# Row-block order 3, 1, 2, 0 with a lag of three steps in two causal attentions, and the forget gate's columns inside the first value chunk

## The chip, the cores and the metric

One core of a Trainium2 chip runs the whole program. The metric is the device time of one execution in microseconds, median of the runs. Engines: TensorE (PE) multiplies and transposes; VectorE (DVE) and ScalarE (ACT) compute elementwise and read the accumulators (PSUM banks); GpSimd (POOL) computes elementwise in SBUF; the SP queue issues the loads. All float32.

## The reference, cut to what matters

Two transformer blocks over 512 tokens of width 1024, batch 1. The change is in the first block:

```python
proj = h @ w_in            # q_a k_a v_a z_a q_b k_b v_b z_b (512 columns each), f_logit (8), g_logit (2048)
# per head (8 heads of 64), 128 query rows at a time, keys up to the block's end (causal)
z = q_a @ k_a.T / 8                                   # stick-breaking attention
log_1m = where(s < t, log_sigmoid(-z), 0)
after = cumsum(log_1m, reverse=True) - log_1m
y_a = where(s < t, exp(log_sigmoid(z) + after), 0) @ v_a
F = cumsum(log_sigmoid(f_logit + b_forget))           # over tokens, per head
y_b = softmax(q_b @ k_b.T / 8 + F[t] - F[s], s <= t) @ v_b    # forgetting attention
y_a, y_b = y_a * silu(z_a), y_b * silu(z_b)           # then output projections, gates, merge
```

Row block b (rows 128b to 128b+127) sees b+1 blocks of keys.

## The kernel before, in words

**Weights.** All weight matrices stream in chunks through three raw slots. For every product `mm3` (L448) does three matmuls, high x high, high x low and low x high; ScalarE makes the high part of a chunk (`split_weights`, L1086, the instruction is L1104), POOL the low part as a difference of two SBUF tiles (`low_weights`, L2294, the instruction is L2301, a quarter of a chunk each). SP loads a slot when it is used up (`chunk_in`, L2346; from chunk 12 on in a loop, L2389). All matmuls have the line L425, all transposes ("turns") L432.

**Before the attentions** TensorE makes q_a, k_a, v_a (in rows: `project_rows`, L504, with chunk 12 the first of two), z_a, q_b and k_b. ScalarE or VectorE move each tile out of its bank (`move`, L1137 and L1810). Then 24 matmuls of 8 x 512 (L604 to L609) make f_logit from w_f, whose parts were split early (L1163, L1786). ScalarE takes it through Abs, Exp and Ln (L1278 to L1285), VectorE through a maximum and a scan over the tokens (L1833, L1834).

**The attentions.** Four head pairs times four row blocks are 16 steps of each; the 32 run in one loop on every engine, step n having pair n // 4 and block n % 4, so lengths 1, 2, 3, 4. On TensorE (L671) step i does in this order:

- the scores of step i (`head_scores`, L621), into one of two pairs of banks, which must be free;
- the turns of the weights of step i - LAG, LAG = 2 (`head_turns`, L635), into the one pair of banks for turns;
- side work: half a tile of the projections v_b, z_b and g (`side`, L658): 18 matmuls of 256 columns or 9 of 512 in an even step, 30 or 15 in an odd one, all into the one bank 7;
- the values of step i - LAG (`head_values`, L644), which need the turned weights copied to SBUF.

ScalarE in the first attention (`stick_step`, L1299): in even steps the side tile's copy, then Abs, Exp, Ln of the scores of i (L1309 to L1311), then the Exp of step i - 1 (L1317) once VectorE is done with it; in steps 4k and 4k+1 half a weight split (L1325, L1327), and in the later even ones the silu of z_b. VectorE (`stick_step`, L1839): after the last block of a pair the gating product (L1845), then the copy of the turned weights of i - LAG (L1812), then the chain of step i: maximum and sum (L1856), two scans from the right, one a head (L1859), and the difference (L1861), which frees the score banks. In even steps from 10 on the silu product (L1817).

In the second attention VectorE does a reduce that also gives the row's extremum (L1891) and the scaling by the reciprocal sum (L1900, L1903), ScalarE the Exp (L1361) and the copy of the turned weights (L1141), beside the gates' work. Weights stand in `pairs`, four slots in the first attention and three in the second; the turned weights in two slots `ptb`. After the last values eight tiles of g follow (L694).

Of the kernel before, what the change touches and what calls it, by code (L numbers as in the profile page):

```python
# [7 lines left out]
F32 = mybir.dt.float32  # L8
# [21 lines left out]
LAG = 2  # L30
SLOTS_A, SLOTS_B = 4, 3
# [25 lines left out]
EARLY_CHUNKS = 12  # L57
# [7 lines left out]
for _n, _c in (("c", 8), ("b_ada", 24), ("norm_g", 8), ("b_gate", 16), ("final_g", 8), ("mix_g", 8),  # L65
# [3 lines left out]
               ("conv_b", 22), ("b_forget", 1), ("w_f", 64), ("lora", 256), ("g2", 256), ("pool_w", 256)):  # L69
# [3 lines left out]
NCOLS = PARAM_COLS["w_f"][0]  # L73
LATE_PARAM = PARAM_COLS["lora"][0]
# [61 lines left out]
def build(nc, x_in, mem_in, params_in, consts_in, ada_in, stream_in, down_in, out, x2_kept, kx_kept, vx_kept, nF_kept):  # L136
    with ExitStack() as ctx:
# [79 lines left out]
        w_raw, w_lo = sb_both("weights", RAW, CHUNK_F)  # L217
        w_hi = sb("weights_high", HI, CHUNK_F, kind=F32R)
# [3 lines left out]
        wf_hi = sb("w_f_high", 64, kind=F32R)  # L222
        wf_lo = sb("w_f_low", 64, kind=F32R)
# [75 lines left out]
        pairs, ptb = at(W1, SLOTS_A, 2, T), at(W1 + 4096, 2, 2, T)  # L299
# [78 lines left out]

        def raw_of(c):
            return h_slots[0][c] if c < 2 else w_raw[:, c % RAW, :]  # L380

        def lo_of(c):
            return h_slots[1][c] if c < 2 else w_lo[:, c % RAW, :]

        def hi_of(c):
            return h_slots[2][c % 2] if c in (0, 1, 4, 5) else w_hi[:, c % HI, :]
# [34 lines left out]
        def _(pe):  # L421
# [82 lines left out]
            def project_rows(key, first, last, lhs, blocks):  # L504

                for i in range(first, last):
                    c, b = divmod(i, blocks)
                    if b == 0:
                        chunk[0] = next_chunk(KD, 256)
# [85 lines left out]
            project_rows("va", 0, 2 * NB, hrow, NB)  # L595
# [39 lines left out]
            def head_turns(tag, n, slots, weights_done):  # L635

                pe.wait_ge(weights_done, n + 1)
                o = TR2.take(pe, ("T" + tag, n))
                for hh in range(2):
                    for s in range(n % NB + 1):  # L640
                        turn(o[hh][:, P * s:P * (s + 1)], pairs[:, n % slots, hh, P * s:P * (s + 1)],
                             TR2.filled if hh and s == n % NB else None)

            def head_values(tag, n, v):  # L644

                pair, b = divmod(n, NB)
                TR2.wait_out(pe, ("T" + tag, n))
                if b == 0:
                    PV.take(pe, ("y" + tag, pair))
                y = bank[6]  # L650
                for s in range(b + 1):
                    for hh in range(2):
# [3 lines left out]
                           PV.filled if b == NB - 1 and s == b and hh else None)  # L656
# [415 lines left out]
        def _(act):  # L1072
# [13 lines left out]
            def split_weights(part=0, parts=1):  # L1086
# [7 lines left out]
                n = (CHUNK_F if c < STREAM else DOWN_K * P) // parts  # L1094
# [68 lines left out]
            high(wf_hi, par("w_f", 0, 64), sem("wf_hi"))  # L1163
# [121 lines left out]
            nc.scalar.activation(fa, fa, ACT.Ln, bias=1.0).then_inc(sem("f_ln"), 1)  # L1285

# [12 lines left out]
            def stick_step(i):  # L1299
# [13 lines left out]
                if 0 <= n < N:  # L1313
                    end = P * (n % NB + 1)
                    M2.wait_out(act, ("a", n))
                    w = pairs[:, n % SLOTS_A, :, 0:end]
# [30 lines left out]
            def fox_step(i):  # L1347
# [4 lines left out]
                if 0 <= n < N:  # L1352
                    end = P * (n % NB + 1)
                    move(("Tb", n), ptb[:, n % 2, :, 0:end], lambda o: o[:, :, 0:end], TR2)
                if i < N:
                    end = P * (i % NB + 1)
                    M2.wait_out(act, ("b", i))
                    for hh in range(2):
                        c = 2 * (i % SLOTS_B) + hh
                        w = pairs[:, i % SLOTS_B, hh, 0:end]  # L1360
                        nc.scalar.activation(w, w, ACT.Exp, scale=-1.0, bias=small[:, 8 + c:9 + c],  # L1361
                                             accum_out=small[:, 14 + c:15 + c]).then_inc(sem("fox_exp"), 1)
# [340 lines left out]
        def _(dve):  # L1703
# [80 lines left out]
            dve.wait_ge(sem("wf_hi"), 1)  # L1784
            tt(gmix[:, :], par("final_g", 0, 8), par("mix_g", 0, 8), ALU.mult)
            tt(wf_lo, par("w_f", 0, 64), wf_hi.bitcast(F32), ALU.subtract).then_inc(sem("wf_split"), 1)  # L1786
# [41 lines left out]
            for m in range(4):  # L1828
                move(("kb", m), kb[:, m, :])

# [4 lines left out]
                .then_inc(sem("nF_ready"), 1)  # L1835


            N = PAIRS * NB
            def stick_step(i):  # L1839
# [7 lines left out]
                if 0 <= n < N:  # L1847
                    end = P * (n % NB + 1)
                    move(("Ta", n), ptb[:, n % 2, :, 0:end], lambda o: o[:, :, 0:end], TR2)
                if i < N:  # L1850
                    end = P * (i % NB + 1)
                    o = M2.full(dve, ("a", i))
                    w = pairs[:, i % SLOTS_A, :, 0:end]
# [660 lines left out]
```

## Time and profile before

| | us |
|---|---|
| median of 3 runs | 1319.56 (1319.38 to 1319.75) |
| the profiled execution | 1318.44 |
| its span | 1316.6 |
| TensorE busy | 1269.6 (96%) |
| VectorE busy | 638.0 (48%) |
| ScalarE busy | 543.6 (41%) |
| POOL busy | 538.7 (41%) |

The profile is one execution. "Busy" is the time with an instruction running; a row of the timeline gives start, length, engine, line, operation, the tiles by name, how many were merged (x), and in brackets the idle time before it with what ended it. A merged group runs in each step: its length is that of all of them. Matmuls are pipelined: the next one starts before the last one's end, so costs on TensorE are differences of starts. The first attention's scores start at 218.7 us, the second's at about 306, and the tiles of g after both at 390.0.

### The profile page before, as it was taken

What the parts mean: (1) busy time and instruction counts of PE and PEld (TensorE: products, weight loads), DVE (VectorE), ACT (ScalarE), POOL (GpSimd) and SP (SyncE); (2) the same over time, 40 slices, a digit from 0 to 9 for tenths busy, and PEclk for the clock granted to TensorE, in tenths of its full rate; (3) what the DMA queues carried; (4) which work ended last, traced back from release to release, by engine and by line L of the source; (5) the groups of instructions that cost most, each with busy time, mean ns of one, the idle gap of its engine ahead of it and who ended that gap; (6) DMA issues with size and microseconds to landing.
All of it is one profiled execution on the core that took longest, in us unless ns stands there. A gap on an engine that the chain in (4) does not pass through costs nothing.

```text
span 1316.6 us, 19858 instructions
## 1 busy us (share of the span) xinstructions
PE 1269.6 (96%) x8194; PEld 1007.3 (77%) x8194; DVE 638.0 (48%) x995; ACT 543.6 (41%) x834; POOL 538.7 (41%) x432
## 2 busy tenths in 40 slices
PE   6999999999999999999999899999999999999999
PEld 5778887766768888766787667778788888888887
DVE  4450002886440166696448647265565656562000
ACT  5541434676665233463544444353422323221111
POOL 6554443131333454364142126421455555544443
PEclk9999999999999999999999999999999999999999
DMA  9835221202112222421220023300222222222223
GB/s 391 331 138 194 97 96 65 81 33 81 64 65 91 87 88 91 186 87 64 80 91 5 3 82 120 150 33 32 96 96 97 96 96 96 96 76 88 88 88 108
DMA packets 20549, 133.26 MB, mean 101 GB/s; under 512 B 2280, under 2 KB 2408, under 8 KB 7408
## 3 DMA queue, kind: packets, MB, share of 16 engines
q1 hardware_dynamic: 18720, 119.50, 25.4%
q10 hardware_dynamic: 1744, 12.53, 2.5%
q8 instruction: 65, 1.06, 0.3%
q14 instruction: 20, 0.16, 0.0%
HBM read 125.71 MB, written 6.31 MB: 100 GB/s over the span
## 4 chain that ended last, share of the span: by engine, by line
PE 86%; DVE 8%; ACT 4%; issue 2%; DMA 0%; POOL 0%; SPq 0%; ACTq 0%; DVEq 0%
PE banks L425 84%; PE banks L432 2%; DVE arena L2005 1%; DVE arena L1859 1%; ACT arena L1141 1%; DVE arena L1969 1%; DVE arena L2004 0%; ACT arena L1310 0%; ACT arena L1309 0%; DMA arena<-in_mem 0%; DVE arena L1812 0%; DVE arena L1856 0%; ACT arena L1311 0%; DVE arena L2031 0%; DVE arena L2030 0%
## 5 line engine op out<-in xcount | busy, mean ns | idle before, releaser
L2301 POOL TENSOR_TENSOR weights_low<-weights,weights_high 128x512 fp32r<-128x512 f32 (+1 forms) x388 | 498.5, 1316 | 669.7 <-ACT weights_high L1104 669.7
L425 PE MATMUL banks<-h_high_low,weights_high 128*128 128x512 f32 x880 | 356.0, 405 | 2.4 <-POOL weights_low L2301 1.3
L425 PE MATMUL banks<-h_high_low,weights_low 128*128 128x512 f32 x880 | 347.6, 395 | 0.0
L425 PE MATMUL banks<-h_low,weights_high 128*128 128x512 f32 x880 | 347.5, 395 | 0.0
L1104 ACT ACTIVATE weights_high<-weights 128x2048 fp32r<-128x2048 f32 (+2 forms) x105 | 178.2, 1697 | 343.4 <-PE banks L425 331.0
L425 PEld LDWEIGHTS banks<-h_high_low,weights_high 128*128 128x128 f32 x880 | 165.2, 188 | 48.4 <-issue 7.1
L425 PEld LDWEIGHTS banks<-h_low,weights_high 128*128 128x128 f32 x880 | 165.2, 188 | 41.0 <-issue 2.9
L425 PEld LDWEIGHTS banks<-h_high_low,weights_low 128*128 128x128 f32 x880 | 164.9, 187 | 40.4
L425 PE MATMUL banks<-arena 64*64 64x64 f32 (+4 forms) x1288 | 104.8, 280 | 15.1 <-DVE arena L1812 6.4
L425 PEld LDWEIGHTS banks<-arena 64*64 64x64 f32 (+3 forms) x1288 | 73.8, 152 | 37.4 <-issue 17.9
L1939 DVE TENSOR_TENSOR xres<-banks,xres 128x512 f32<-128x512 f32 x24 | 16.6, 690 | 141.2 <-PE banks L425 141.2
L425 PE MATMUL banks<-gact_high,weights_high 128*128 128x512 f32 x176 | 69.6, 396 | 0.0
L425 PE MATMUL banks<-gact_low,weights_high 128*128 128x512 f32 x176 | 69.6, 396 | 0.0
L425 PE MATMUL banks<-gact_high,weights_low 128*128 128x512 f32 x176 | 69.6, 395 | 0.0
L1141 ACT ACTIVATE arena<-banks 128x256 f32<-128x256 f32 (+4 forms) x82 | 41.6, 519 | 66.6 <-PE banks L432 33.6
L1812 DVE COPY arena<-banks 128x256 f32<-128x256 f32 (+3 forms) x40 | 25.4, 635 | 78.1 <-PE banks L425 74.3
L425 PE MATMUL banks<-weights_high,h_high_low 128*128 128x256 f32 x192 | 55.1, 287 | 0.3 <-ACT arena L1141 0.3
L425 PE MATMUL banks<-weights_low,h_high_low 128*128 128x256 f32 x192 | 53.9, 281 | 0.0
L425 PE MATMUL banks<-weights_high,h_low 128*128 128x256 f32 x192 | 53.9, 281 | 0.0
L2273 DVE TENSOR_TENSOR arena<-banks,sums 128x512 f32<-128x512 f32 x22 | 15.2, 692 | 77.3 <-PE banks L425 72.2
L1124 ACT ACTIVATE sums<-xres 128x512 f32<-128x512 f32 x32 | 20.2, 632 | 70.4 <-DVE xres L1939 39.4
L432 PE MATMUL banks<-consts,arena 128*128 128x128 f32 x245 | 38.0, 281 | 2.8 <-DVE arena L2231 2.7
(347 smaller groups left out, 2045.6 us busy)
## 6 DMA issues: line engine op xcount, KB each, us to landing
weights<-in_stream SPq DMA_DIRECT2D x83, 1024.0 KB, 4.9
weights<-in_down SPq DMA_DIRECT2D x16, 704.0 KB, 4.0
arena<-in_ada SPq DMA_DIRECT2D x8, 1024.0 KB, 12.3
arena<-in_ada SPq DMA_DIRECT2D x8, 512.0 KB, 7.3
h<-in_stream SPq DMA_DIRECT2D x2, 1024.0 KB, 9.1
xres<-in_x SPq DMA_DIRECT2D x1, 2048.0 KB, 28.5
x_kept<-xres ACTq DMA_DIRECT2D x1, 2048.0 KB, 6.3
xres<-x_kept ACTq DMA_DIRECT2D x1, 2048.0 KB, 7.8
```

Source lines behind the costliest of these rows:

```text
L425: ins = nc.tensor.matmul(o, lhsT, rhs, start=start, stop=stop, skip_group_check=skip)
L432: ins = nc.tensor.transpose(o, i, ident[0:rows, 0:rows])
L1104: nc.scalar.activation(hi_of(c)[:, cols], raw_of(c)[:, cols], ACT.Copy)\
L1124: nc.scalar.activation(SQ[n][i % 2][:, 0:width], src[:, k, 0:width], ACT.Square)\
L1141: nc.scalar.activation(dst, s_, ACT.Copy).then_inc(ring_.out(key), 1)
L1812: nc.vector.tensor_copy(dst, o if src is None else src(o)).then_inc(ring_.out(key), 1)
L1859: ins = nc.vector.tensor_tensor_scan(v, ones(end), v, 0.0, ALU.mult, ALU.add)
L1939: ins = tt(xres[:, m, :], o, xres[:, m, :], ALU.add)
L1969: tt(dst, o, zscale, ALU.mult).then_inc(M.out(key), 1)
L2005: stt(zm[:, m, :], zdiff, par("mu", m), z[:, 1:T + 1], ALU.mult, ALU.add).then_inc(sem("zm"), 1)
L2273: tt(a[:, 2:T + 2], o, rms[:, :], ALU.mult).then_inc(M.out(("up", m, 0)), 1)
L2301: nc.gpsimd.tensor_tensor(lo_of(c)[:, cols], raw_of(c)[:, cols], hi_of(c)[:, cols].bitcast(F32), ALU.subtract).then_inc(sem("weights_split ...
```

## The change

- `ROW_ORDER = (3, 1, 2, 0)`: in both attentions the blocks of a pair go in this order, so lengths 4, 2, 3, 1, on every engine; the first block of a pair in the new order does the pair's waits, the last one signals its end.
- LAG = 3; four slots of weights in both attentions (the fourth is in `sums`).
- The eight columns of w_f lie behind the first 256 columns of v_a: chunk 12 has 264 columns per row tile. Its 96 matmuls make 264 columns; ScalarE copies the last eight of each of the four row tiles to `f_cols` and waits for that copy before the main one. After q_b TensorE turns the four [128 x 8] tiles into f_logit's [8 x 512] (before k_b). The 24 matmuls and the split of w_f are gone.
- ScalarE's forget chain comes before two weight splits, VectorE's before the four moves of k_b.
- SP issues chunks 12 to 14 by hand, before the late parameters; slot 0 of the weights is 2112 columns wide and the others 2048.

```diff
-LAG = 2
-SLOTS_A, SLOTS_B = 4, 3
+LAG = 3
+SLOTS_A, SLOTS_B = 4, 4
+ROW_ORDER = (3, 1, 2, 0)
...
-EARLY_CHUNKS = 12
+EARLY_CHUNKS = 15
+WITH_F, F_WIDE = 12, 256 + HEADS
...
-        pairs, ptb = at(W1, SLOTS_A, 2, T), at(W1 + 4096, 2, 2, T)
+        pairs = [at(W1 + 1024 * i, 2, T) for i in range(3)] + [sums[:, 0:2, :]]
+        ptb = at(W1 + 4096, 2, 2, T)
...
-            def project_rows(key, first, last, lhs, blocks):
+            def project_rows(key, first, last, lhs, blocks, wide=256):
...
+                    n = wide if c == 0 else 256
...
-                        mm3(o[:, 0:256], lhs(k, b), [p_[:, k, :] for p_ in w], k == 0, k == KD - 1,
+                        mm3(o[:, 0:n], lhs(k, b), [p_[:, k, :] for p_ in w], k == 0, k == KD - 1,
...
             project("qb", 4, KD, h, T)
+            o = M.take(pe, "f")
+            pe.wait_ge(sem("f_cols"), NB)
+            for b in range(NB):
+                turn(o[0:HEADS, P * b:P * (b + 1)], f_cols[:, b, :], M.filled if b == NB - 1 else None)
             project("kb", 4, KD, h, T)
-            o = M.take(pe, "f")
-            pe.wait_ge(sem("wf_split"), 1)
-            wf = [v.rearrange("p (k n) -> p k n", k=KD) for v in (wf_hi, wf_lo)]
-            for k in range(KD):
-                mm3(o[0:HEADS, :], [v[:, k, :] for v in wf], h(k), k == 0, k == KD - 1,
-                    M.filled if k == KD - 1 else None)
...
-                pair, b = divmod(i, NB)
-                if b == 0:
+                pair, b = i // NB, ROW_ORDER[i % NB]
+                if i % NB == 0:
...
                 for i in range(first, last):
                     c, b = divmod(i, NB)
+                    if c == 0:
+                        o = M.full(act, (key, c, b))
+                        nc.scalar.activation(f_cols[:, b, :], o[:, 256:F_WIDE], ACT.Copy).then_inc(sem("f_cols"), 1)
+                        act.wait_ge(sem("f_cols"), b + 1)
...
-            for _ in range(2):
-                split_weights()
-
             o = M.full(act, "f")
             fx, fa = z_gate[0:HEADS, 0, :], z_gate[0:HEADS, 1, :]
+            act.wait_ge(sem("silu"), 4)
...
             nc.scalar.activation(fa, fa, ACT.Ln, bias=1.0).then_inc(sem("f_ln"), 1)
+            for _ in range(2):
+                split_weights()
...
-                    end = P * (i % NB + 1)
-                    e = pairs[:, i % SLOTS_A, :, 0:end]
+                    end = P * (ROW_ORDER[i % NB] + 1)
+                    e = pairs[i % SLOTS_A][:, :, 0:end]
...
-            for m in range(4):
-                move(("kb", m), kb[:, m, :])
-
             fx, fa = z_gate[0:HEADS, 0, :], z_gate[0:HEADS, 1, :]
             dve.wait_ge(sem("f_ln"), 1)
             link(stt(fx, fx, 0.0, fa, ALU.max, ALU.add))
             nc.vector.tensor_tensor_scan(nF[0:HEADS, :], ones(T, HEADS), fx, 0.0, ALU.mult, ALU.add)\
                 .then_inc(sem("nF_ready"), 1)
+            for m in range(4):
+                move(("kb", m), kb[:, m, :])
...
-            for c in range(8, EARLY_CHUNKS):
+            for c in range(8, WITH_F):
                 chunk_in(c)
             for k in range(ADA_RING, KD):
                 gate_in(k)
+            for c in range(WITH_F, EARLY_CHUNKS):
+                chunk_in(c)
             sp.dma_start(params[:, LATE_PARAM:], params_in[:, LATE_PARAM:]).then_inc(sem("late_loaded"), 16)
```

## Rows read from the trace of the kernel before

**Rows 1.** The page: the chain of work that ended last, shares of the span by engine.

```profile
PE 86%; DVE 8%; ACT 4%; issue 2%; DMA 0%; POOL 0%; SPq 0%; ACTq 0%; DVEq 0%
```

**Rows 2.** Who TensorE waited for: total, times, longest (whole span; then 365.5 to 389).

```profile
PE banks L425 <- DVE arena L1812: 6.4, 4, 2.0
...
PE banks L425 <- ACT arena L1141: 2.0, 2, 1.1
```

**Rows 3.** TensorE by 2 us windows: length, busy (count), granted clock, DMA share, GB/s.

```profile
282.00:284.00 2.00, 0.23 (x4) 1.00 0.21 86
...
304.00:306.00 2.00, 0.10 (x2) 1.00 0.25 102
306.00:308.00 2.00, 2.00 (x18) 0.67 0.00 0
308.00:310.00 2.00, 2.00 (x11) 0.50 0.03 8
```

**Rows 4.** Timeline of TensorE: four turns; first and last of 24 forget matmuls.

```profile
166.76 0.60 PE L432 MATMUL banks<-consts,arena 128*128 128x128 f32 x4
167.12 0.48 PE L425 MATMUL banks<-h_high_low,weights_high 128*128 128x512 f32 x1
...
212.00 0.39 PE L425 MATMUL banks<-h_high_low,w_f_high 128*8 128x512 f32 x1
...
217.32 0.40 PE L425 MATMUL banks<-h_high_low,w_f_low 128*8 128x512 f32 x1
```

**Rows 5.** Timeline of TensorE in the second period of the first attention.

```profile
241.82 1.04 PE L432 MATMUL banks<-consts,arena 128*128 128x128 f32 x8
...
242.62 0.36 PE L425 MATMUL banks<-weights_high,h_high_low 128*128 128x256 f32 x1
...
246.35 1.94 PE L425 MATMUL banks<-arena 128*64 128x128 f32 x20
...
248.35 0.39 PE L432 MATMUL banks<-consts,arena 128*128 128x128 f32 x2
248.49 0.36 PE L425 MATMUL banks<-weights_high,h_high_low 128*128 128x256 f32 x1
...
250.79 1.50 PE L425 MATMUL banks<-arena 128*64 128x128 f32 x8
...
252.34 0.61 PE L432 MATMUL banks<-consts,arena 128*128 128x128 f32 x4
```

**Rows 6.** Timeline: ScalarE starts a 3-block step; VectorE's copy behind its chain.

```profile
227.16 0.81 ACT L1309 ACTIVATE arena<-banks 128x768 f32<-128x768 f32 x1 [0.47 <-PE banks L425]
...
233.54 0.68 DVE L1812 COPY arena<-banks 128x512 f32<-128x512 f32 x1
```

**Rows 7.** The chain of waits, 252 to 262 us, a 4-block step: start, length, what.

```profile
252.54 1.03 ACT arena L1309
...
254.69 1.07 ACT arena L1311
...
257.11 2.35 DVE arena L1859 x2
...
260.63 0.96 DVE arena L1812
...
261.63 0.43 PE banks L425 x3
```

**Rows 8.** Timelines of ScalarE, VectorE and POOL where VectorE and POOL meet.

```profile
243.31 0.64 ACT L1311 ACTIVATE arena<-arena 128x512 f32<-128x512 f32 x1
...
244.78 2.34 DVE L1859 TENSOR_TENSOR_SCAN arena<-consts,arena 128x256 f32<-128x256 f32 x2
...
245.28 2.90 POOL L2301 TENSOR_TENSOR weights_low<-weights,weights_high 128x512 fp32r<-128x512 f32 x2 [1.30 <-ACT weights_high L1104]
...
312.50 2.61 DVE L1903 TENSOR_SCALAR arena<-arena,small 128x128 f32<-128x128 f32 x2
...
312.51 2.51 POOL L2301 TENSOR_TENSOR weights_low<-weights,weights_high 128x512 fp32r<-128x512 f32 x2 [2.91 <-ACT weights_high L1104]
```

More of the change, by code:

```diff
@@ L72 @@
 NPARAM = _at
-NCOLS = PARAM_COLS["w_f"][0]
-LATE_PARAM = PARAM_COLS["lora"][0]
+NCOLS = LATE_PARAM = PARAM_COLS["lora"][0]
 CONST_COLS = {}
@@ L638, in head_turns @@
                 o = TR2.take(pe, ("T" + tag, n))
+                b = ROW_ORDER[n % NB]
                 for hh in range(2):
-                    for s in range(n % NB + 1):
-                        turn(o[hh][:, P * s:P * (s + 1)], pairs[:, n % slots, hh, P * s:P * (s + 1)],
-                             TR2.filled if hh and s == n % NB else None)
+                    for s in range(b + 1):
+                        turn(o[hh][:, P * s:P * (s + 1)], pairs[n % slots][:, hh, P * s:P * (s + 1)],
+                             TR2.filled if hh and s == b else None)
             def head_values(tag, n, v):
-                pair, b = divmod(n, NB)
+                pair, b = n // NB, ROW_ORDER[n % NB]
                 TR2.wait_out(pe, ("T" + tag, n))
-                if b == 0:
+                if n % NB == 0:
                     PV.take(pe, ("y" + tag, pair))
@@ L655, in head_values @@
                            ptb[:, n % 2, hh, P * s:P * (s + 1)], s == 0, s == b,
-                           PV.filled if b == NB - 1 and s == b and hh else None)
+                           PV.filled if n % NB == NB - 1 and s == b and hh else None)
             def side(i):
@@ L1093, in split_weights @@
                     return
-                n = (CHUNK_F if c < STREAM else DOWN_K * P) // parts
+                n = width_of(c) // parts
                 cols = slice(n * part, n * (part + 1))
@@ L1313, in stick_step @@
                 if 0 <= n < N:
-                    end = P * (n % NB + 1)
+                    end = P * (ROW_ORDER[n % NB] + 1)
                     M2.wait_out(act, ("a", n))
-                    w = pairs[:, n % SLOTS_A, :, 0:end]
+                    w = pairs[n % SLOTS_A][:, :, 0:end]
                     nc.scalar.activation(w, w, ACT.Exp).then_inc(sem("stick_w"), 1)
@@ L1359, in fox_step @@
                         c = 2 * (i % SLOTS_B) + hh
-                        w = pairs[:, i % SLOTS_B, hh, 0:end]
+                        w = pairs[i % SLOTS_B][:, hh, 0:end]
                         nc.scalar.activation(w, w, ACT.Exp, scale=-1.0, bias=small[:, 8 + c:9 + c],
-                                             accum_out=small[:, 14 + c:15 + c]).then_inc(sem("fox_exp"), 1)
+                                             accum_out=small[:, 16 + c:17 + c]).then_inc(sem("fox_exp"), 1)
                 if i in (5, 9):
@@ L1847, in stick_step @@
                 if 0 <= n < N:
[L1848 removed]
+                    end = P * (ROW_ORDER[n % NB] + 1)
                     move(("Ta", n), ptb[:, n % 2, :, 0:end], lambda o: o[:, :, 0:end], TR2)
                 if i < N:
[L1851 removed]
+                    end = P * (ROW_ORDER[i % NB] + 1)
                     o = M2.full(dve, ("a", i))
[L1853 removed]
+                    w = pairs[i % SLOTS_A][:, :, 0:end]
                     dve.wait_ge(sem("stick_ln"), i + 1)
@@ L1879, in fox_step @@
                 if i < N:
-                    pair, b = divmod(i, NB)
-                    end = P * (b + 1)
-                    if b == 0:
+                    pair = i // NB
+                    end = P * (ROW_ORDER[i % NB] + 1)
+                    if i % NB == 0:
                         dve.wait_ge(sem(f"nF{pair % 2}_loaded"), 16 * (pair // 2 + 1))
@@ L1890, in fox_step @@
                         c = 8 + 2 * (i % SLOTS_B) + hh
-                        ins = nc.vector.tensor_tensor_reduce(pairs[:, i % SLOTS_B, hh, 0:end], o[:, hh, 0:end],
+                        ins = nc.vector.tensor_tensor_reduce(pairs[i % SLOTS_B][:, hh, 0:end], o[:, hh, 0:end],
                                                              nF_bc[pair % 2][:, hh, 0:end], -1.0, 3.0e38, ALU.add, ALU.min,
@@ L1896, in fox_step @@
                 if 0 <= n < N:
-                    end = P * (n % NB + 1)
+                    end = P * (ROW_ORDER[n % NB] + 1)
                     c = 2 * (n % SLOTS_B)
                     dve.wait_ge(sem("fox_exp"), 2 * n + 2)
-                    link(nc.vector.reciprocal(small[:, 48 + c:50 + c], small[:, 14 + c:16 + c]))
+                    link(nc.vector.reciprocal(small[:, 48 + c:50 + c], small[:, 16 + c:18 + c]))
                     for hh in range(2):
-                        w = pairs[:, n % SLOTS_B, hh, 0:end]
+                        w = pairs[n % SLOTS_B][:, hh, 0:end]
                         ins = ts(w, w, small[:, 48 + c + hh:49 + c + hh], None, ALU.mult)
```

51 lines of the change are left out of this document (27 added, 24 removed).

## The prediction

> **What bounds the kernel now.** I read the page's chain of waits first, then who waited for whom on TensorE (PE), then the timelines of the three engines in both attentions. TensorE is 86% of the chain that ended last [rows 1]: time is gained only where TensorE gets less to do or waits less. In the region that the change touches it waits for VectorE's copies L1812 four times, 6.4 us in all, twice 2.0 and so twice about 1.2, all in the first (stick-breaking) attention; and twice for ScalarE's copies at the end of the second, 2.0 us in all [rows 2]. Inside the second attention there is no such wait. So 8.4 us of waiting can be won there at most, plus what the clock cost: behind one of the two 2.0 us waits the granted clock was 0.67 for 2 us and 0.50 (the 1.2 GHz level) for 2 more, which loses 0.66 + 1.0 = 1.7 us; behind the other, just as long, it stayed at 1.00 [rows 3].
>
> **Part 1, the forget gate.** Removed: 24 matmuls of 512 columns, started 212.00 to 217.32, 23 steps of 0.231, so 5.55 us of TensorE [rows 4]. Added: the 96 matmuls of the first value chunk go from 256 to 264 columns. Twelve 256-column matmuls are the difference between the long and the short side part, 3.73 and 2.30 us (from the starts 242.62, 246.35, 248.49, 250.79), so 0.119 each [rows 5]; 512 columns take 0.231, so a column costs 0.44 ns and the eight more cost 96 x 3.5 ns = 0.34 us. Four turns of [128 x 8]: four full turns took 166.76 to 167.12, 0.36 us, and 0.1 more for the refilled pipe [rows 4]. Bounds of this part: 4.5 (if turns and wide matmuls cost twice as much) and 5.1. I take 5.55 - 0.34 - 0.46 = **-4.8 us**.
>
> What rides along is covered. ScalarE's four small copies with a wait each stand beside row tiles of 24 x 0.119 = 2.8 us of TensorE, of which ScalarE's one copy fills a small part; the split of chunk 12 is 3% longer. If the cover were gone the four would cost under 0.81 us each, what ScalarE takes for 768 columns of a bank [rows 6]. ScalarE's forget chain now runs while TensorE works on the first key tile (24 x 0.231 = 5.6 us), and the two weight splits queued behind it are not wanted before the side work. VectorE's max and scan go ahead of the four key copies; the last of these, which releases the bank that the first scores take, is not late. The SP queue issues chunks 12 to 14 by hand in the old order; the late parameters come behind them and are first read hundreds of microseconds later. The removed high/low split of w_f was off the chain: nothing gained.
>
> **Part 2, order and lag.** Numbers of a step n mean: position 4k holds 4 blocks, 4k+1 two, 4k+2 three, 4k+3 one. TensorE's work is the same; what counts is where VectorE's copy of the turned weights (L1812, three steps late) stands: in program order behind the whole chain of the step before. A 4-block chain runs from Abs at 252.54 over the scans at 257.11 to the copy at 260.63, and TensorE goes on at 261.63: 9.09 us, here with a 3-block copy [rows 7]. In the new order the 3-block copy of 4k+2 stands behind the chain of 4k+4 likewise. TensorE meanwhile does: turns of 2, side 2.30, values 2 with scores 2, turns of 3, side 3.73. Turns go from 0.14 (1 block) to 0.80 (4), so 0.36 and 0.58; values and scores together 2.00 for 7 blocks and 1.55 for 5, so 1.33 for 4 [rows 5]. Sum 8.30: a wait of **0.8** each period, three times, 2.4. The 4-block copy of 4k stands behind the 3-block chain of 4k+2: 227.16 to 233.54 is 6.38 [rows 6], with the gating product (0.6, an estimate: two thirds of the 0.96 of a 768-column copy [rows 7]) and the copy itself (1.2, estimate from the same) 8.2 to 8.3; TensorE does 0.14 + 2.30 + 0.88 + 0.80 + 3.73 = 7.85: **0.4**, three times, 1.3 with the first pair's smaller one. The silu products of the last periods delay VectorE as they do now, by 0.8 (from 1.2 to 2.0 [rows 2]), at three of these places: 2.4. Sum 6.1 against 6.4 now: the order moves the waits, it doesn't remove them.
>
> At the start the first chain is now a long one. Scores of step 2 need the bank that step 0's chain releases, 8.2 us after its scores; TensorE has 2.30 + 0.73 + 3.73 = 6.8 to do: 1.5 us. Then step 2's side work wants the side bank, whose ScalarE copy is queued behind the exponential of the long block: 0.6. Start: **+2.1**. At the end three steps of turns and values stand without side work, not two, with a ScalarE copy before each and gate work between: bounds 2.0 (as now) and 3.3 (three of the longest, 1.1 [rows 2]); I take 2.9, **+0.9**. Attention without anything else: 6.1 + 2.1 + 2.9 - 8.4 = **+2.7**, bounds +1.7 and +4.
>
> **The collision.** ScalarE splits a half chunk right after the Ln and a short Exp of each step 4k and 4k+1, and POOL then runs two subtractions. Now 4k is the shortest step; in the new order it is the 4-block one, on the chain that TensorE waits for. In the trace scan pairs that meet POOL are slow: two 256-column scans took 2.34 while POOL's pair took 2.90 from 245.28 [rows 8], where two 512-column scans took 2.35 undisturbed, so about 1.2 was expected [rows 7]. The loss of 1.1 costs nothing today (VectorE waits for ScalarE afterwards). Where POOL asked within 0.01 us of VectorE (312.51, 312.50), two tiny products took 2.61 [rows 8]. Timing of the meeting: with the same short Exp between, POOL starts 245.28 - 243.95 = 1.33 us after Ln's end [rows 8]; the long block's scans start 257.11 - 255.76 = 1.35 after it [rows 7]. They meet head on, in three periods (k = 1 to 3). Price per meeting 1.1 (scan first, one subtraction in between) to 2.3 (both scans held). I take 1.5, nearer the low end since the starts are a tie: **+4.5**, bounds 3.4 and 6.9.
>
> The Trainium skill, SBUF — State Buffer, section Who interferes with whom, says that VectorE with two SBUF inputs and GpSimd share one pair of ports by an exclusive lock, and the loser is blocked for the whole instruction. The rows above agree; it speaks against this change, and by it the scans (constant ones and a tile) are always hit, the copies from PSUM never. Without the rule and its rows the sum would stand at -2.1 before the clock.
>
> **Clock.** The waits at 4k+2 become 2.3, 2.3 and about 3. A 2.0 us wait lowered the clock once in two [rows 3]. Between 0 and three or four losses of 1.7; I take two, 3.4, against 1.7 now: **+1.7**. The Trainium skill, TensorE: Matmul & The Clock Gate, section What's actually happening, calls the observation free-running, which would make the count a matter of phase; the two equal waits agree.
>
> **Sum.** -4.8 + 2.7 + 4.5 + 1.7 = +4.1 us. The profiled execution took 1318.44 (span 1316.6), 1.1 below the median of the runs, 1319.56; I lay the difference on both: 1322.5 for a profiled one, **1323.7** for the median.
>
> **The rivals.** (1) *No collision on the chain*, faster: VectorE and POOL slip past each other (ScalarE's Exp ahead of the split is held, or the scans come first and POOL's pair fits behind). Then -4.8 + 2.7 and the clock between 0 and -1.7: -2.9, **1316.7**. For it: the tie is 0.02 us wide. Against: POOL's pair lasts 2.5 us and the scans 2.35, so they overlap unless one is 2 us off. It decides when the extra per period is under about 0.3. (2) *The third step of slack covers every copy*, as the lag suggests: -4.8 - 6.4 - 1.7 + 0.9 = -12, **1307.6**. Against it: a later use doesn't help a copy whose place in VectorE's queue moved just as far; it would need chains 2 us shorter than those of [rows 6, 7]. (3) *The small collision*: 1.1 a meeting and one drop of the clock: -4.8 + 2.7 + 3.4 + 0 = +1.3, **1320.9**, no difference.
>
> **How the numbers follow.** A measurement of this kernel tells 0.2%, 2.6 us, from no change. Collision with its price near or over my value: 0.50, slower. Rival 3: 0.25, same. Rival 1: 0.18, of which 0.13 faster and 0.05 same. Rival 2: 0.07, faster. So faster 0.20, same 0.30, slower 0.50. Range: the collision's upper bound with two drops is 1319.56 - 4.8 + 2.7 + 6.9 + 1.7 = 1326.1, with one more drop 1327.8; below it reaches rival 1: 1316.5 to 1327.5. Of the cases with a collision alone it would be 1320.5 to 1327.5. Outside stay rival 2, the clock-free half of rival 1 and a tail above, under 0.2.
>
> **What would show it.** Right: the forget matmuls gone and the first scores 4.8 us earlier; waits for L1812 at the values of 4k+2 of 2 us and more from the second pair on, 0.8 in the first; L1859 pairs of 512 columns at 3.4 to 4.6 us beside L2301 three times, 2.35 the first time; a bank wait of 1.5 us before the third scores; three waits at the end; granted clock 0.5 behind some of them. Wrong: 512-column scans all at 1.2, or L1812 waits under 3 us in all.

## The result, and the profile after

The changed kernel took 1328.76 us (median of six runs, 1325.78 to 1331.14), the kernel before in the same comparison 1319.95 (1319.38 to 1322.32). The ratio is 1.006, 95% interval 1.0048 to 1.0072: about 8 us slower, where +4.1 was forecast. No run lies near the median: three took 1325.78 to 1326.96 us and three 1330.57 to 1331.14. The profiled execution took 1326.96 with a span of 1325.4, 8.8 us above the span before. Three landmarks split these 8.8 us (us from the start of the span):

| | first scores | first g tile behind both attentions | end | start moved | attentions | rest |
|---|---|---|---|---|---|---|
| before | 218.72 | 389.99 | 1316.6 | | 171.3 | 926.6 |
| after | 214.27 | 394.71 | 1325.4 | -4.45 | 180.4 (+9.2) | 930.7 (+4.1) |

The chain of work that ended last is still TensorE's, with a point more of VectorE, against [rows 1]:

```profile
PE 84%; DVE 9%; ACT 4%; issue 2%; DMA 0%; POOL 0%; SPq 0%; ACTq 0%; DVEq 0%
```

Who TensorE waited for between 205 and 312 us of the changed kernel, and then between 385 and 402 (total, times, longest), against 6.4 and 2.0 in [rows 2]:

```profile
PE banks L433 <- DVE arena L1822: 12.8, 7, 3.7
PE banks L433 <- DVE arena L1871: 1.6, 1, 1.6
PE banks L433 <- ACT arena L1149: 0.4, 1, 0.4
```

```profile
PE banks L433 <- ACT arena L1149: 2.5, 3, 1.4
```

L1822 is the copy that was L1812. Of its 12.8 us, 1.0 stands before the first scores, where the kernel before waited 1.0 for ScalarE. So 16.4 us of waiting stand in the attentions, in 11 waits, where 8.4 stood in 6. The three largest are the ones behind the long chains. Timeline of VectorE in the changed kernel, around the second long block and then the two later ones:

```profile
220.22 2.37 DVE L1869 TENSOR_TENSOR_SCAN arena<-consts,arena 128x512 f32<-128x512 f32 x2
...
238.67 1.22 DVE L1866 SCALAR_TENSOR_TENSOR arena<-banks,arena 128x1024 f32<-128x1024 f32 x1 [2.17 <-ACT arena L1323]
239.93 4.51 DVE L1869 TENSOR_TENSOR_SCAN arena<-consts,arena 128x512 f32<-128x512 f32 x2
244.47 1.23 DVE L1871 TENSOR_TENSOR arena<-banks,arena 128x1024 f32<-128x1024 f32 x1
245.61 0.95 DVE L1822 COPY arena<-banks 128x768 f32<-128x768 f32 x1
...
263.81 4.51 DVE L1869 TENSOR_TENSOR_SCAN arena<-consts,arena 128x512 f32<-128x512 f32 x2
...
288.30 4.52 DVE L1869 TENSOR_TENSOR_SCAN arena<-consts,arena 128x512 f32<-128x512 f32 x2
```

And the same moment on ScalarE, POOL and TensorE:

```profile
237.51 1.06 ACT L1323 ACTIVATE arena<-arena 128x1024 f32<-128x1024 f32 x1
...
238.47 0.40 ACT L1329 ACTIVATE sums<-sums 128x256 f32<-128x256 f32 x1
238.78 1.04 ACT L1112 ACTIVATE weights_high<-weights 128x1024 fp32r<-128x1024 f32 x1
...
239.90 3.45 POOL L2311 TENSOR_TENSOR weights_low<-weights,weights_high 128x512 fp32r<-128x512 f32 x2 [19.51 <-ACT weights_high L1112]
...
246.61 1.72 PE L433 MATMUL banks<-arena 128*64 128x128 f32 x16 [3.00 <-DVE arena L1822]
...
270.50 1.72 PE L433 MATMUL banks<-arena 128*64 128x128 f32 x16 [3.13 <-DVE arena L1822]
...
295.60 2.38 PE L433 MATMUL banks<-arena 128*64 128x128 f32 x16 [3.75 <-DVE arena L1822]
```

Read it from the right: TensorE has stood 3.00 us when the copy of 245.61 is through; that copy is queued behind the whole chain, and in the chain two scans take 4.51 us that took 2.37 the first time, where POOL's last subtraction ended 0.2 us after their start. POOL starts its two subtractions at 239.90, 0.03 us ahead of the scans. The same happens in each of the three later periods: 2.15 us each, 6.5 in all.

The start and the end show the smaller terms, TensorE's timeline again:

```profile
223.90 0.92 PE L433 MATMUL banks<-arena 64*128 64x384 f32 x4 [1.58 <-DVE arena L1871]
...
225.47 0.39 PE L433 MATMUL banks<-weights_high,h_high_low 128*128 128x256 f32 x1 [0.44 <-ACT arena L1149]
...
389.80 0.66 PE L433 MATMUL banks<-arena 128*64 128x128 f32 x8 [0.69 <-ACT arena L1149]
...
392.63 0.88 PE L433 MATMUL banks<-arena 128*64 128x128 f32 x12 [1.36 <-ACT arena L1149]
...
394.34 0.44 PE L433 MATMUL banks<-arena 128*64 128x128 f32 x4 [0.47 <-ACT arena L1149]
```

The clock, in 2 us windows (length; busy time and count of TensorE's matmuls, its weight loads, VectorE, ScalarE and POOL; granted clock, DMA share, GB/s), fell once behind the longest wait, and once where it had not before, in the second block of the program, far behind the change:

```profile
294.00:296.00 2.00, 0.40 (x8) 0.40 (x10) 2.00 (x4) 1.89 (x2) 0.00 (x0) 1.00 0.02 4
296.00:298.00 2.00, 2.00 (x16) 0.76 (x13) 1.97 (x3) 0.60 (x2) 1.81 (x2) 0.63 0.03 8
298.00:300.00 2.00, 2.00 (x8) 1.71 (x9) 1.49 (x3) 1.62 (x2) 1.55 (x1) 0.52 0.00 0
...
716.00:718.00 2.00, 2.00 (x62) 1.88 (x66) 0.99 (x2) 1.89 (x5) 0.00 (x0) 0.59 0.00 0
718.00:720.00 2.00, 2.00 (x64) 1.66 (x60) 1.52 (x6) 0.00 (x0) 0.00 (x0) 0.56 0.03 8
```

The two windows of each lose 0.74 + 0.96 = 1.7 us and 0.82 + 0.88 = 1.7 us.

### The profile page after: what moved, and what is told of

Its sections match the earlier page's. It is cut to its first block, busy times and chain, and to the rows that moved or that the text cites. A ratio compares the mean times of both kernels' runs of the same rounds, so it can differ in the third digit from the quotient of the medians.

```text
span 1325.4 us, 19815 instructions
## 1 busy us (share of the span) xinstructions
PE 1270.3 (96%) x8174; PEld 1010.1 (76%) x8174; DVE 640.1 (48%) x994; ACT 543.4 (41%) x837; POOL 542.9 (41%) x432
## 4 chain that ended last, share of the span: by engine, by line
PE 84%; DVE 9%; ACT 4%; issue 2%; DMA 0%; POOL 0%; SPq 0%; ACTq 0%; DVEq 0%
PE banks L433 83%; DVE arena L1869 2%; PE banks L440 1%; DVE arena L2015 1%; ACT arena L1149 1%; DVE arena L1822 1%; DVE arena L1866 1%; ACT arena L1322 1%; ACT arena L1323 1%; DVE arena L1979 1%; ACT arena L1321 0%; DVE arena L2014 0%; DMA arena<-in_mem 0%; DVE arena L2041 0%; DVE arena L2040 0%
## 5 line engine op out<-in xcount | busy, mean ns | idle before, releaser
L2311 POOL TENSOR_TENSOR weights_low<-weights,weights_high 128x512 fp32r<-128x512 f32 (+2 forms) x388 | 502.8, 1329 | 672.2 <-ACT weights_high L1112 672.2
L1112 ACT ACTIVATE weights_high<-weights 128x2048 fp32r<-128x2048 f32 (+3 forms) x105 | 178.3, 1698 | 341.5 <-PE banks L433 341.5
L433 PE MATMUL banks<-arena 64*64 64x64 f32 (+6 forms) x1288 | 104.7, 280 | 21.6 <-DVE arena L1822 12.8
L1149 ACT ACTIVATE arena<-banks 128x512 f32<-128x512 f32 (+5 forms) x82 | 41.5, 518 | 52.9 <-PE banks L440 29.4
L433 PE MATMUL banks<-weights_high,h_high_low 128*128 128x256 f32 (+1 forms) x192 | 55.3, 288 | 0.7 <-ACT arena L1149 0.7
L433 PE MATMUL banks<-weights_low,h_high_low 128*128 128x256 f32 (+1 forms) x192 | 54.2, 282 | 0.0
L433 PE MATMUL banks<-weights_high,h_low 128*128 128x256 f32 (+1 forms) x192 | 54.2, 282 | 0.0
L1822 DVE COPY arena<-banks 128x256 f32<-128x256 f32 (+3 forms) x40 | 25.3, 633 | 55.7 <-PE banks L433 46.8
L433 PEld LDWEIGHTS banks<-gact_low,weights_high 128*128 128x128 f32 x176 | 33.0, 188 | 8.6
## 6 DMA issues: line engine op xcount, KB each, us to landing
arena<-in_ada SPq DMA_DIRECT2D x8, 1024.0 KB, 11.9
```

Source lines behind the costliest of these rows:

```text
L433: ins = nc.tensor.matmul(o, lhsT, rhs, start=start, stop=stop, skip_group_check=skip)
L1112: nc.scalar.activation(hi_of(c)[:, cols], raw_of(c)[:, cols], ACT.Copy)\
L1149: nc.scalar.activation(dst, s_, ACT.Copy).then_inc(ring_.out(key), 1)
L1822: nc.vector.tensor_copy(dst, o if src is None else src(o)).then_inc(ring_.out(key), 1)
L2311: nc.gpsimd.tensor_tensor(lo_of(c)[:, cols], raw_of(c)[:, cols], hi_of(c)[:, cols].bitcast(F32), ALU.subtract).then_inc(sem("weights_split ...
```

## The experiments

The theory, **collision**: POOL's two subtractions and the scans of the long block meet head on in three periods, which costs 2.15 us each plus what the longer waits take from the clock; the row order does nothing else of weight (too strong, as experiments 1 and 3 show), and the third step of lag gives nothing, since the copy moved just as far in VectorE's queue (**queue**). The rivals: the meeting is incidental, and the order or ScalarE's split on the long chain is to blame; or the lag is what costs or helps. Unless another base is named, an edit is made to the changed kernel. Ratios are to the kernel before.

**1. The splits moved.** Only the first half chunk's split leaves the step of the long block for the end of the step before it, in both attentions:

```diff
-                if i % 4 == 0 and 4 <= i <= N:
+                if i % 4 == 3 and i < N:
                     split_weights(0, 2)
```

> The changed kernel with one thing moved on ScalarE: the first half of each weight split in the attentions goes from step 4k to the end of step 4k-1, so that POOL's two subtractions are over before the scans of the 4-block step; the second half stays in 4k+1. Theory 'collision': the three scan pairs of 4.51 us are 2.35 again, the copies L1822 are waited for 0.8 to 1.5 us instead of 3.0, 3.1 and 3.7, the clock's drop near 296 us goes with them: about 7 to 10 us under the changed kernel, 0.996 to 1.000 of the kernel before. Rival 'order and lag alone' (the long chain and its queued copy make the waits, POOL has no part): waits of 3 us stay, ratio 1.005 to 1.007.

Measured: 1320.76 us, ratio 1.0001 (0.9991 to 1.001). VectorE's timeline, and then who TensorE waited for (205 to 402 us):

```profile
239.20 2.34 DVE L1869 TENSOR_TENSOR_SCAN arena<-consts,arena 128x512 f32<-128x512 f32 x2
```

```profile
PE banks L433 <- DVE arena L1822: 7.1, 7, 1.6
PE banks L433 <- ACT arena L1149: 3.0, 4, 1.2
PE banks L433 <- DVE arena L1871: 1.6, 1, 1.6
```

All four long pairs are back at 2.3 to 2.4, and 5.7 of the 12.8 us of waiting for the copy are gone. Moving POOL's work off the long scans is worth 0.6%, about 8 us, as much as the changed kernel had lost. The waits give 5.6 of these 8 (17.4 and 11.7 us between 205 and 402), and the profile has no loss of the clock before 1315 us, where the changed kernel's had two.

**2. The same move in the kernel before.** If moving the split is good in itself, it is good here too; if it is the meeting that counts, the move should now do harm, since the long block stands at 4k+3.

> The same move in the kernel before (order 0, 1, 2, 3, lag 2). There step 4k+3 is the 4-block one, so the move puts POOL's pair onto its scans. Theory 'collision': four scan pairs of 512 columns at 3.5 to 4.6 us, L1812 waited for 2 us and more in the first periods too, 4 to 8 us slower, ratio 1.003 to 1.006. Rival 'order and lag alone': nothing changes, ratio 0.999 to 1.001.

Measured: 1328.85 us, ratio 1.0054 (1.0041 to 1.0067). VectorE's scans and POOL's pair:

```profile
235.20 3.39 DVE L1859 TENSOR_TENSOR_SCAN arena<-consts,arena 128x512 f32<-128x512 f32 x2
...
235.84 3.82 POOL L2301 TENSOR_TENSOR weights_low<-weights,weights_high 128x512 fp32r<-128x512 f32 x2 [17.06 <-ACT weights_high L1104]
```

The edit that mends the changed kernel spoils the old one: in all four periods the long pair takes 3.4 us. Here the first scan is already running when POOL asks, and one subtraction gets in between, +1.05; in the changed kernel POOL is first, and two get in, +2.15. The meeting is not all of this loss, though. The waits for the copies L1812 grew by 2.5 us (6.4 to 8.9), those for ScalarE in the attentions by 3.0 (2.0 to 5.0; its split moved in the second attention too), and the clock was lost three times instead of once. What the meeting alone costs here was not separated.

**3. The forget gate alone**, and **4. the order, lag and slots alone.** The first is the changed kernel with the old values of the constants; the second is the kernel before with the new ones.

```diff
-LAG = 3
-SLOTS_A, SLOTS_B = 4, 4
-ROW_ORDER = (3, 1, 2, 0)
+LAG = 2
+SLOTS_A, SLOTS_B = 4, 3
+ROW_ORDER = (0, 1, 2, 3)
```

> Only the forget gate's part (columns inside the first value chunk, chains moved forward), with order 0, 1, 2, 3, lag 2 and 4 and 3 slots. Both theories: 4.8 us less TensorE work and the attentions as before: ratio 0.9958 to 0.9970, 1314 to 1316 us. If part of it comes back (later clock drops, or the key tiles' moves late) 0.997 to 0.999.

> Only the order 3, 1, 2, 0 with lag 3 and four slots, the forget gate as before. Theory 'collision': 9 us longer attentions by the three waits, the start and the end, and the clock: ratio 1.008 to 1.012. If the two parts work on each other (rival: the earlier start shifts ScalarE's split onto the scans) it would be less, 1.002 to 1.006, and the scan pairs would be 2.35 to 3.5.

Measured: the forget gate 1318.66 us, 0.9971 (0.996 to 0.9982), a gain of 3.8 us (2.7 by the medians, 1318.66 against 1321.38); order, lag and slots 1332.9 us, 1.0078 (1.0065 to 1.0091), a loss of 10.3. The product of the two ratios is 1.0049, the lower end of what both together gave: the parts don't act on each other in a way that shows. In the second the long scans stand at 4.51, 4.51 and 4.53 us, and TensorE waits 11.9 us for the copy. Experiment 1, measured beside experiment 3, says what order and lag cost without the meeting: 1.0001 against 0.9971, and the intervals don't touch. That is 2 to 4 us, and the profiles have 11.7 and 9.2 us of waiting (205 to 402 us).

**5. The lag alone, 6. the order without the lag.** Experiment 5 takes ROW_ORDER back to (0, 1, 2, 3) and leaves lag 3 and the four slots; experiment 6 leaves the new order and sets LAG = 2.

> The changed kernel with the old order 0, 1, 2, 3 and the lag of three kept: against the run with the forget part alone it adds only the lag. Theory 'queue' (the copy of the turned weights stands in VectorE's order behind the chain of the step before, so a later use moves its place too): one wait of about 1.5 us a pair at the 2-block values instead of the 3-block ones, scans of 4 blocks 2.35 us, the sum of VectorE waits 5 to 7 us as with lag two: ratio 0.996 to 0.998. Rival 'slack': the copy has a step more and the waits vanish, 0.991 to 0.993.

> The changed kernel with lag two: the order alone beside the forget part. Theory 'collision': the 4-block scans meet POOL three times (4.5 us), now one wait of 2.5 to 3.3 us a pair from the second on, at the 1-block values behind that chain; some 4 us over the forget part alone: ratio 1.000 to 1.004. Rival 'the lag does the harm': as the forget part alone, 0.996 to 0.998.

Measured: 5 took 1317.01 us, 0.998 (0.9967 to 0.9992), no better than the 0.9971 of experiment 3, which has lag 2 and three slots of weights in the second attention and is otherwise the same. A row of the waits (205 to 402 us) and one of TensorE's timeline say why: TensorE waits in every period again, and as long for the copy as with lag 2 (7.2 us in five waits in experiment 3):

```profile
PE banks L433 <- DVE arena L1822: 7.3, 6, 1.6
```

```profile
234.87 1.29 PE L433 MATMUL banks<-arena 128*64 128x128 f32 x12 [1.44 <-DVE arena L1822]
```

Experiment 6 took 1326.09 us, 1.0039 (1.0023 to 1.0055), with the three long pairs at 4.5 us: most of the loss belongs to the order, not to the lag. Against the change with lag 3 (1.006) the intervals overlap, so a cost of the third step is not shown by the times. The profiles have 12.9 us of waiting with lag 2 and 17.4 with lag 3 (205 to 402 us), so the third step adds waits beside the collision rather than covering them.

**7. Values alone a step later.** What would make a step of slack real? The copy must stand ahead of the next chain and its use a step behind it. So turns and copies stay two steps behind, and values alone go to three; the splits are moved as in experiment 1.

```diff
-LAG = 3
+LAG, VLAG = 2, 3
...
-            for i in range(2 * N + LAG):
+            for i in range(2 * N + VLAG):
...
-                elif n >= N:
+                elif N <= n < 2 * N:
                     head_turns("b", n - N, SLOTS_B, sem("fox_w"))
...
+                n = i - VLAG
                 if 0 <= n < N:
                     head_values("a", n, va)
```

(VectorE's two output gates and its loop take VLAG where they had LAG.)

> A version meant to beat both: order 3, 1, 2, 0, the turns two steps behind and only the values three, so that the copy between them has a step of its own, and the first half of the splits moved as in e1. Theory 'queue' plus 'collision': scans of 4 blocks 2.35 us, VectorE waits in the first attention under 2.5 us in all beside the 1.5 us at the start: ratio 0.991 to 0.994, 1309 to 1312 us. Rival: VectorE itself is full in the first attention (18 to 19 us of work in a pair of 20), so the waits only move: 0.996 to 0.998.

Measured: 1312.45 us, ratio 0.9935 (0.992 to 0.995), the fastest of all, 0.65% ahead of the kernel before. Who TensorE waited for, 205 to 402 us; L1823 is the copy:

```profile
PE banks L433 <- DVE arena L1872: 1.6, 1, 1.6
PE banks L433 <- DVE arena L1856: 1.1, 2, 0.8
PE banks L433 <- DVE arena L1823: 1.0, 1, 1.0
PE banks L440 <- issue: 0.7, 1, 0.7
PE banks L433 <- ACT arena L1150: 0.2, 1, 0.2
```

The one wait left for the copy is the 1.0 before the first scores. The attentions take 166.5 us (214.35 to 380.86), 4.8 less than before.

**8. The same with the old order, 9. POOL alone held back, 10. experiment 7 with the splits where they were.** Experiment 8 keeps the order (0, 1, 2, 3) and the splits. Experiment 9 asks which of the two partners of the meeting matters, ScalarE's split or POOL's subtractions: ScalarE does what it does in the changed kernel, and only POOL waits until the long chain has released its bank:

```diff
+                    if c in (22, 23, 24):
+                        M2.wait_out(pool, ("a", 4 * (c - 21)))
                     for i in range(PIECES):
```

> Order 0, 1, 2, 3 with turns two steps behind and values three, splits where they were, forget part kept. Theory 'queue': the waits of 1.1 to 2.0 us fall to under 0.5 each, the scans of 4 blocks stay clear of POOL; start without the bank wait; one longer wait where the second attention begins: ratio 0.992 to 0.995. Rival as in e7: 0.996 to 0.998.

> The changed kernel with POOL alone held: its subtractions of the chunks 22, 23 and 24 wait until VectorE has freed the scores of the 4-block steps 4, 8 and 12; ScalarE's and all other orders stay. Theory 'collision' (POOL's subtraction on the scans is the cost, not ScalarE's half split in that step): scan pairs 2.35 us, waits for L1822 0.8 to 1.6 us, ratio 0.999 to 1.001 like e1. Rival 'ScalarE's split is in the way': waits of 3 us stay, 1.005 to 1.007.

> As e7 (order 3, 1, 2, 0, turns two steps behind, values three) but with the half splits where the changed kernel has them. Theory 'collision': the 4-block scans take 4.5 us three times again, and since the chain also holds the score banks the slack for the copies doesn't help: TensorE waits about 1.8 us for the banks (L1872) three times and 0.7 for the side bank; 6 to 9 us over e7, ratio 0.998 to 1.001. Rival 'slack hides it': as e7, 0.993 to 0.995.

Measured: 8 took 1313.85 us, 0.9945 (0.993 to 0.996). So nearly all that experiment 7 gains comes with the old order as well; between the two the intervals overlap. Experiment 9 took 1319.39 us, 0.9995 (0.9983 to 1.0006), VectorE and POOL at the place where they met:

```profile
240.03 2.34 DVE L1869 TENSOR_TENSOR_SCAN arena<-consts,arena 128x512 f32<-128x512 f32 x2
...
243.71 5.77 POOL L2313 TENSOR_TENSOR weights_low<-weights,weights_high 128x512 fp32r<-128x512 f32 x4 [23.21 <-DVE arena L1871]
```

ScalarE's split still stands in the long chain's step, the scans take 2.34, and the loss is gone: it is POOL's subtractions beside the scans, not ScalarE's time. The meeting itself has only moved. The held subtractions now fall on the 256-column scans of the next step:

```profile
245.13 3.27 DVE L1869 TENSOR_TENSOR_SCAN arena<-consts,arena 128x256 f32<-128x256 f32 x2
```

These took 1.27 us at this place in the changed kernel, so 2.0 us are lost here, nearly as much as before. But this chain is short, and the waits for the copy fall from 12.8 us to 7.3 all the same. Experiment 10 took 1319.97 us, 0.9997 (0.9988 to 1.0006). The meeting costs the good version as much as it cost the change. VectorE and POOL:

```profile
240.43 4.51 DVE L1870 TENSOR_TENSOR_SCAN arena<-consts,arena 128x512 f32<-128x512 f32 x2
...
240.40 3.46 POOL L2312 TENSOR_TENSOR weights_low<-weights,weights_high 128x512 fp32r<-128x512 f32 x2 [19.38 <-ACT weights_high L1113]
```

And who TensorE waited for:

```profile
PE banks L433 <- DVE arena L1872: 6.5, 4, 1.7
```

The copy is in time now, so the chain's 2.15 us come out elsewhere: the scores wait for the bank that L1872 releases, four times instead of once.

**11, 12. Both kernels profiled again**, unedited, on one chip, for the 4.1 us of the rest that no term of mine had.

> The kernel before, profiled a second time on another chip; nothing is edited. Asked: the program behind both attentions was about 4 us longer in the one profile of the changed kernel (930.7 us from the first tile behind the attentions to the end, 926.6 before), which no part of the change explains. Theory 'kernel': the extra belongs to the changed program (its later part meets TensorE's unexplained waits, 3.6 us between 680 and 720 us against 1.4, and a second drop of the clock at 716 us), so this profile repeats 926.6 within 0.5 and 1.4. Rival 'execution': these waits and the clock vary from one execution to the next, and this profile shows 928 us or more and 2.5 us or more of such waits.

> The changed kernel, profiled a second time on the same chip as the kernel before; nothing is edited. Theory 'kernel': 930 to 931 us behind the attentions again, with the clock below 0.65 near 716 us. Rival 'execution': another sum; the clock falls elsewhere or once more. Either way the three pairs of 512-column scans take 4.5 us each, since instructions and their order are the same, and the wait for the copy behind them is 3.0 us or more each time.

Measured, one execution each: 1320.66 us (span 1318.8) and 1332.16 (span 1330.6). The attentions of the kernel before took 171.3 us again (219.19 to 390.48) and its rest 928.3, with 2.5 us of waits at 680 to 720 us that the profile doesn't explain, where the first profile had 1.4. The changed kernel's attentions took 185.2 us this time (215.22 to 400.40), its rest 930.2. Its long scans and the waits behind them repeat to the hundredth:

```profile
242.33 4.51 DVE L1869 TENSOR_TENSOR_SCAN arena<-consts,arena 128x512 f32<-128x512 f32 x2
...
249.01 2.04 PE L433 MATMUL banks<-arena 128*64 128x128 f32 x16 [3.00 <-DVE arena L1822]
```

The clock does not. Windows (columns as in the result) behind the first and the last of the five places where it fell between 226 and 404 us, one behind each of the five longest waits:

```profile
226.00:228.00 2.00, 1.57 (x7) 1.57 (x8) 1.40 (x3) 1.94 (x4) 0.00 (x0) 0.60 0.02 4
228.00:230.00 2.00, 2.00 (x12) 2.00 (x11) 1.03 (x2) 1.35 (x2) 0.00 (x0) 0.55 0.00 0
...
398.00:400.00 2.00, 1.53 (x12) 0.80 (x10) 0.00 (x0) 0.69 (x3) 2.00 (x2) 0.50 0.00 0
400.00:402.00 2.00, 2.00 (x8) 1.38 (x7) 1.48 (x3) 1.87 (x4) 1.43 (x2) 0.50 0.04 8
402.00:404.00 2.00, 2.00 (x7) 1.56 (x6) 2.00 (x4) 0.00 (x0) 0.00 (x0) 0.53 0.00 0
```

Its mean clock is 0.991, a loss of 0.009 x 1330.6 = 12 us, about seven times 1.7 (the last of the five places counts twice, and one more lies at 700.8 us), where the first profile lost 1.7 twice. The span grew by 5.2 only, about 1 us for each loss more. Waits that are 0.9 us shorter (16.5 against 17.4 us between 205 and 402) explain a part of that; the rest is open.

As for the rest of the program, part of its growth is a loss of the clock: in the second pair 1.7 us near 700 us and 1.7 more because the low stretch at 397 to 404 us reaches over the landmark at 400.40. But part belongs to the changed program. The same 1002 matmuls of the second block, undisturbed in every profile, before and after:

```profile
986.56:1219.89 233.33, 233.33 (x1002) 1.00 0.26 91
```

```profile
994.36:1228.54 234.18, 234.18 (x1002) 1.00 0.26 91
```

The stretch takes 233.33 us in all four profiles with the old forget gate (the two of the kernel before, experiments 2 and 4) and 234.18 in all ten with the new one, whatever the order and the lag. Over the last 5800 matmuls, but for 1800 of them from about 690 to 750 us, the four take 858.8 to 859.4 us and the ten 860.8 to 861.2: 2.0 us more that come with the forget gate's part. Which piece of it does this was not tried; SBUF addresses moved with the wider slot and w_f. The 1800 matmuls left out take 58.1 to 61.6 us, with up to 3.4 of clock losses and 2.4 to 5.2 of waits that the profile doesn't explain, in no order that follows the edit. So theory "kernel" has 2.0 us and rival "execution" the remainder. A clock loss between 680 and 720 us stands in five of the ten profiles and in none of the four; whether that is the edit's doing stays open.

## Why the prediction was right or wrong

The direction was right, and its first cause, the meeting in three periods. The size was half of what came, and two steps failed that carry the miss: the clock's term, with a range that used only part of its own count, and the rest of the program put at nothing. For the first pair of profiles (+8.8) the terms compare so:

| | forecast | measured |
|---|---|---|
| start, forget gate | -4.8 | -4.45 |
| waits in the attentions | +7.2 | +8.0 |
| attentions beside the waits | 0 | +1.2 |
| clock, both losses of a pair's profile counted | +1.7 | +1.7 |
| rest without the clock | 0 | +2.4 |

Point by point, in its own terms:

- **Forget gate, -4.8**: the first scores came 4.45 us earlier (4.0 in the second pair of profiles), and alone the part gained 3.8 us by the ratio, 2.4 to 5.3 by its interval. The four turns cost 0.35 us (190.17 to 190.52), and the four small copies of 0.178 us each stood in idle time of ScalarE. As a cost before the attentions the term is right, a few tenths too good. Its lower bound is not: turns and wide matmuls at twice their cost give 5.55 - 0.68 - 0.92 = 3.95, not 4.5. And the part brings 2.0 us more behind 400 us, which the term left out.
- **Waits without the collision, 11.1 us in all**: at the start 1.5 + 0.6 forecast, 1.58 + 0.44 measured; at the end 2.9 forecast, 2.5 measured. For the copies of 4k, 2.9 forecast with their share of the silu products, 2.0 measured. Rival 2, the third step of slack, is refuted by the waits and by experiment 5: a copy's place in VectorE's queue moves with its use.
- **Collision, +4.5**: found in the right three periods. The Trainium skill, SBUF — State Buffer, section Who interferes with whom, has the pair of VectorE and GpSimd lock each other out; 2.37 against 4.51 us for the same scans, and experiment 9, agree. **Its price was mis-sized**: "I take 1.5, nearer the low end since the starts are a tie" measured 2.15, three times. The working had the order of the start (1.33 us against 1.35 behind Ln) and it came out so, POOL 0.03 ahead; I then hedged it away. With 2.15 in place of 1.5 the forecast waits at 4k+2 become 2.95, 2.95 and 3.75, against 3.00, 3.13 and 3.75 measured. This is 2.0 us of the miss, of which the terms above, 1.4 us smaller than forecast, give most back.
- **Left out**: waits went from 6 to 11 and from 8.4 to 16.4 us, 8.0 more, while the attentions grew by 9.2 with one clock loss in either. The other 1.2 may be TensorE's pipe filling again behind five more waits; this was not tried by itself.
- **Clock, +1.7**, the step that put the median outside the range. "Between 0 and three or four losses of 1.7; I take two" fits the first profile. But the six runs fall in two groups: mean clock 0.997 to 0.999 with 1325.78 to 1326.96 us, inside the range, and 0.993 with 1330.57 to 1331.14. At 0.993 the loss is 0.007 x 1329 = 9 us, five or six drops; the second profile shows seven, at the start and the end too, where the prediction counted none. Two waits of equal length of which one lowered the clock gave a chance of a half each; on the five longest waits (1.58, 3.00, 3.13, 3.75 and 1.36) that is two or three losses in the middle and five at the upper end. The range didn't even use the term's own bounds: "two drops", "one more drop 1327.8", and then 1327.5. With four losses (+5.1) and the upper bounds of the other terms (-4.5, +4, +6.9) it would have ended at 1331.1. The price was off the other way: the groups lie some 4.7 us apart for four or five drops more, so about 1 us for a drop and not 1.7. That the median came out at 1328.76, halfway between the groups, is chance: one run more in the lower group would have put it inside the range. The Trainium skill, TensorE: Matmul & The Clock Gate, section What's actually happening, calls the observation free-running; two against seven losses in two profiles of one program, with the same long waits, agree.
- **Rest of the program, 0**: +1.9 to +4.1 in the two pairs of profiles. 2.0 of it comes with the forget gate's part in every profile; 1.7 in the first pair is a loss of the clock at a place that the change doesn't touch. The prediction had no term for it and gave no reason.

Rival 1 (no collision, 1316.7) is what experiments 1 and 9 built, and by their ratios they came to 1319.7 and 1318.9 on the scale of the forecast, 2 to 3 us above it. The 2.0 us in the rest of the program are most of that.

## What to carry to other kernels

Before a step is moved, look at which engine works beside its new place, not only at what it waits for: VectorE's scans were held for the full length of one or two of POOL's subtractions, and moving POOL's trigger by one step was worth 0.6% here and cost 0.5% in the kernel before. The meeting needn't vanish: in experiment 9 it cost 2.0 us on a short chain, and the program was as fast as before. A later use gives slack to a copy only if the copy keeps its place in its engine's queue: put the producer ahead of the next chain and let only the consumer go later. Where waits of 1.5 us and more are made or removed, give the clock a term of its own for each of them, and compare several runs with their clocks. Compare stretches far behind the edit as well: 1002 untouched matmuls took 0.85 us longer in every profile with the new forget gate.

## What the runs showed of the hardware

- The meeting has a price for each order of arrival: two 512-column scans take 2.34 us alone, 3.40 with POOL 0.40 to 0.64 us behind their start, and 4.51 with POOL 0.03 us ahead. That is one and two subtractions, of about 1.07 us each, let in. The 3.4 came in all four meetings of experiment 2, the 4.5 in all twelve of experiments 4, 6 and 10 and of the changed kernel's first profile.
- One program whose long waits were the same to the hundredth of a microsecond lost the clock twice in one execution and seven times in another, 1.7 us of full clock each; the time grew by about 1 us for each.
- Losses of the clock also stand hundreds of microseconds behind the change, at 716 us in one profile of the changed kernel and at 701 in the other. That the shift of the timeline brought them there is not shown.
- The same 1002 matmuls of 512 columns took 233.33 us in four profiles and 234.18 in ten, by the program's version alone; why is not shown.
